# A two-block transformer kernel: first weight panels of the feed-forward part and of the layers in buffers of their own, third layer panel loaded right behind the first

## What is computed

```python
def first_block(x, ...):
    mix = _token_mixer(_rms_norm(h, pre_mix_g), w_in, ..., w_out)
    h = h + _rms_norm(mix, post_mix_g)
    ffn = _channel_mixer(_rms_norm(h, pre_ffn_g), w_up, ffn_conv_w, ffn_conv_b, w_down)
    return h + _rms_norm(ffn, post_ffn_g)

def _channel_mixer(hn, w_up, ffn_conv_w, ffn_conv_b, w_down):
    f = jnp.einsum('btd,df->btf', hn, w_up)            # 1024 -> 2 * 2816
    f = _causal_dwconv(f, ffn_conv_w) + ffn_conv_b
    gate, up = jnp.split(f, 2, axis=-1)
    return jnp.einsum('btf,fd->btd', jax.nn.gelu(gate) * up, w_down)

def second_block(x, ...):
    for l in range(2):
        h = _rms(x, norm_g[l])
        proj = h @ w_in[l]      # gq gk gv ga gz bq bk bv iq ik iw bz cq ck cv cz gate
        ...                     # linear attention, top-k attention, differential attention
        x = x + merged @ w_out[l]
```

## Time and profile before

| | |
|---|---|
| median of 3 runs | 1924.64 us (1924.58 to 1929.13) |
| profiled execution | 1927.01 us, its span 1925.3 us |
| granted TensorE clock, mean of the span | 0.999 |
| TensorE busy | 98% of the span |
| VectorE, ScalarE busy | 60%, 39% |
| from HBM | 157.59 MB, 83 GB/s over the span |

### The profile page before, as it was taken

How to read it: one execution, slowest core, us unless ns; L and a number is a source line. 1 busy time by engine, 2 the same in 40 slices (tenths; PEclk the granted TensorE clock), 3 DMA queues, 4 the chain that set the end, 5 groups by cost and what they waited for, 6 DMA issues and landing times.

```text
span 1925.3 us, 30380 instructions
## 1 busy us (share of the span) xinstructions
PE 1891.2 (98%) x12689; PEld 1533.5 (80%) x12689; DVE 1159.2 (60%) x1725; ACT 750.9 (39%) x1088; POOL 32.0 (2%) x72
## 2 busy tenths in 40 slices
PE   8999999999999999999999999999999999999999
PEld 5677879888888888787777788888787777778887
DVE  5855565776674363547687944545446678864534
ACT  5633333422222254433444334334533445334421
POOL 3000000110000000000000000000000000000000
PEclk9999999999999999999999999999999999999999
DMA  4211014233333322222223222332222222222232
GB/s 155 92 57 47 25 47 132 80 96 104 94 92 105 110 77 88 73 81 88 66 66 109 69 75 66 99 121 77 88 68 87 77 66 78 92 83 66 66 110 88
DMA packets 166020, 161.65 MB, mean 84 GB/s; under 512 B 13876, under 2 KB 150362, under 8 KB 165882
## 3 DMA queue, kind: packets, MB, share of 16 engines
q1 hardware_dynamic: 165184, 158.99, 26.4%
q10 hardware_dynamic: 698, 0.71, 0.1%
HBM read 157.59 MB, written 2.10 MB: 83 GB/s over the span
## 4 chain that ended last, share of the span: by engine, by line
PE 78%; DVE 2%; ACT 1%; issue 0%; ACTq 0%; DVEq 0%
PE psum L617 64%; PE psum L2128 6%; PE psum L2623 2%; PE psum L2600 1%; PE psum L607 1%; PE psum L2580 1%; PE psum L2608 1%; PE psum L533 1%; DVE w_lo L403 1%; PE psum L542 0%; ACT w_hi L352 0%; PE psum L2704 0%; DVE h_lo L467 0%; PE psum L2689 0%; DVE w_lo L384 0%; PE psum L2657 0%
## 5 line engine op out<-in xcount | busy, mean ns | idle before, releaser
L617 PE MATMUL psum<-h_hi,w_hi 128*128 128x512 f32 (+1 forms) x1568 | 608.2, 388 | 10.9 <-DVE h_lo L467 6.3
L617 PE MATMUL psum<-h_lo,w_hi 128*128 128x512 f32 (+1 forms) x1568 | 594.4, 379 | 0.0
L617 PE MATMUL psum<-h_hi,w_lo 128*128 128x512 f32 (+1 forms) x1568 | 594.4, 379 | 0.0
L403 DVE TENSOR_TENSOR w_lo<-w_raw,w_hi 128x2048 fp32r<-128x2048 f32 (+1 forms) x142 | 297.1, 2092 | 283.0 <-ACT w_hi L352 280.5
L352 ACT ACTIVATE w_hi<-w_raw 128x2048 fp32r<-128x2048 f32 (+1 forms) x142 | 249.3, 1756 | 366.2 <-PE psum L617 295.8
L617 PEld LDWEIGHTS psum<-h_hi,w_hi 128*128 128x128 f32 x1568 | 294.4, 188 | 88.6 <-issue 16.3
L617 PEld LDWEIGHTS psum<-h_hi,w_lo 128*128 128x128 f32 x1568 | 294.5, 188 | 55.8
L617 PEld LDWEIGHTS psum<-h_lo,w_hi 128*128 128x128 f32 x1568 | 294.7, 188 | 52.4
L617 PE MATMUL psum<-w_hi,h_hi 128*128 128x512 f32 (+1 forms) x512 | 183.0, 357 | 0.0
L617 PE MATMUL psum<-w_lo,h_hi 128*128 128x512 f32 (+1 forms) x512 | 179.0, 350 | 0.0
L617 PE MATMUL psum<-w_hi,h_lo 128*128 128x512 f32 (+1 forms) x512 | 178.9, 349 | 0.0
(11 more groups left out here) (371 smaller groups left out, 2203.9 us busy)
## 6 DMA issues: line engine op xcount, KB each, us to landing
w_raw<-in_w_in_dram SPq DMA_DIRECT2D x170, 512.0 KB, 4.4
w_raw<-in_w_up_dram SPq DMA_DIRECT2D x44, 512.0 KB, 5.0
w_raw<-in_w_out_dram SPq DMA_DIRECT2D x24, 512.0 KB, 4.6
w_raw<-in_w_br_dram SPq DMA_DIRECT2D x48, 256.0 KB, 3.0
w_raw<-in_w_down_dram SPq DMA_DIRECT2D x22, 512.0 KB, 4.4
x_first<-in_x_dram SPq DMA_DIRECT2D x4, 512.0 KB, 5.5
x_tokens<-in_x_dram SPq DMA_DIRECT2D x4, 512.0 KB, 4.8
out_dram<-x_tokens SPq DMA_DIRECT2D x4, 512.0 KB, 2.6
```

Of the source, the lines that this page charges most:

```text
L403: eng.eng.tensor_tensor(m.wl[:, g % 2, 0:n], m.raw[:, g % 2, 0:n], m.wh[:, g % 2, 0:n].bitcast(F32), ALU.subtract).then_inc(eng.done, 1)
L617: last = pe.eng.matmul(out, a(k), b(k), start=(opens and k == 0 and i == 0), stop=(k == kt - 1 and i == 2), skip_group_check=ks is not None)
```

## The change

It gives the first panels of the feed-forward part and of each layer buffers of their own, in SBUF areas that other tiles have left by then.

- Feed-forward part, panels 0 and 1: `up_raw`, `up_hi`, `up_lo` (raw and lo share their place). They are loaded behind the mixer's last w_out panel and split between the mixer's last steps, by two new functions, `spare_hi` and `spare_lo`. TensorE does the transposes of tiles 2 and 3 before the last output tile of panel 1 instead of behind it.
- Feed-forward part, panels 2 and 3: loaded as soon as w_out panels 16 and 17 are split; panel 2 is split at the end of the seam, panel 3 behind the first gelu.
- Layers, panels 0, 1 and 2: `first_raw`, `spare_hi`, `spare_lo`. The loads are issued in the order 0, 2, 1. For the first layer all three are split around the last two down panels; for the second layer in the seam, at the places where panels 0 and 1 were split before, and panel 2 behind them in one piece.
- Layers, panels 3 and 4 are loaded into the common slots that the previous part's last panels have left, and split right behind the seam.
- First layer: `iq[1]` (panel 2) is also done in two halves, the first behind the transposes of tiles 2 and 3. In both layers its PSUM banks are 3 and 5 instead of 0 and 1.

```diff
+def spare_hi(act, first, g, i):
+    raw, hi, _ = first[i]
+    act.wait_ge(*act.point(("w raw", g + i)))
+    act.wait_ge(act.done, act.so_far())
+    act.eng.activation(hi[:, :], raw[:, :], ACT.Copy).then_inc(act.done, 1)
+    act.counted(("w hi", g + i))
...
             if p == NP - 1:
+                E.wait_ge(pe_done, E.at(("score 23 mm", TT - 1)))
+                E.wait_ge(pe_done, E.at(("score 1 mm", TT - 1)))
+                E.wait_ge(pe_done, E.at(("turn bk", TT - 1, 1)))
+                for i in range(2):
+                    if i:
+                        E.wait_ge(pe_done, E.at(("y mm", 2 * TT - 1)))
...
+                    E.moved(("w raw", NP + i), f"up_loaded{i}", 2)
                 E.wait_ge(dve_done, E.at(("mix", TT - 1)))
...
         y_root(TT - 1)
+        spare_hi(E, m.first_up, NP, 0)
         mix_hi(1, 3, 3, 4)
+        spare_hi(E, m.first_up, NP, 1)
         split_hi_halves(E, m, 16, KT * PW)
         split(17)
...
         mix_lo(1, 3, 3, 4, (3,))
+        spare_lo(E, m.first_up, NP, 0)
         split_lo_halves(E, m, NPROJ + 2, KT * PW)
         split(NPROJ + 3)
+        spare_lo(E, m.first_up, NP, 1)
...
-        for p in range(FT):
-            E.wait_ge(*E.point(("w lo", base + p - 2)))
+        for p in range(2, FT):
+            E.wait_ge(*E.point(("w lo", base + p - (4 if p < 4 else 2))))
...
                 E.wait_ge(*E.point(("w lo", base + p)))
-                for i in range(2):
-                    up(p, i, tt, half == 1)
-            if half == 0:
-                seam_turn(E, m, banks, seam, 2)
-                seam_turn(E, m, banks, seam, 3)
+                up(p, 0, tt, half == 1)
+                if half == 0 and p == 1:
+                    seam_turn(E, m, banks, seam, 2)
+                    seam_turn(E, m, banks, seam, 3)
+                up(p, 1, tt, half == 1)
...
+            if kk == DN - 2:
+                E.wait_ge(dve_done, E.at(("g lo", 7)))
+                for i in (0, 2):
+                    spare_hi(E, m.first, down_base + DN, i)
         split_hi_halves(E, m, down_base + DN - 1, PANEL)
+        spare_hi(E, m.first, down_base + DN, 1)
...
+    def slot_user(p):
+        return base + p - {3: 4, 4: 6}.get(p, 2)
...
+        if p == iq[1]:
+            return 3 + 2 * i
...
-        for p in range(NP):
-            E.wait_ge(*E.point(("w lo", base + p - 2)))
+        for p in (0, 2, 1, *range(3, NP)):
+            if p == 0 and l == 0:
+                E.wait_ge(dve_done, E.before(None, ("G", FT - 1)))
+            if p == 0 and l:
+                E.wait_ge(dve_done, E.before(l - 1, ("dsa lo", NH - 1)))
+            if p >= 3:
+                E.wait_ge(*E.point(("w lo", slot_user(p))))
...
                 panel(lows, half=1)
+                panel(iq[1], half=1 if seam.post is not None else None)
...
                 seam_turn(E, m, banks, seam, 3)
-        panel(iq[1])
+                panel(iq[1], half=0)
```

111 lines of the change are left out of this document (83 added, 28 removed).

## The result

| | before | after | ratio of the runs, 95% interval |
|---|---|---|---|
| first chip, median | 1924.73 us (4 runs) | 1910.97 us (4 runs, 1909.74 to 1911.81) | 0.9915, 0.9904 to 0.9927 |
| second chip, median | 1929.13 us (13 runs) | 1912.66 us (4 runs) | 0.9917, 0.9902 to 0.9932 |
| third chip, median | 1928.34 us (7 runs) | 1912.21 us (4 runs) | 0.9918, 0.9903 to 0.9933 |

A forecast was written before the change was run, and what follows sets the result against it. TensorE, busy 98% of the span, was taken as the bound, with at most 34 us in waits. 4.7 + 0.5 + 6.3 + 1.7 = 13.2 us, less 0.2, from the median of 1924.64 gave 1911.6 us; range 1909.0 to 1915.5.

The forecast's parts named there:

- First seam, 4.7 + 0.5 us: Mixer to feed-forward: second half starts at 356.87 instead of 361.61 (4.7 us); the third panel's wait goes (0.5 us).
- the very slack of the prediction: First seam: h_lo there at 356.68, TensorE's second half at 356.87, so in time by 0.2 us.
- Second seam, 6.3 us: Feed-forward to first layer: four waits go (5.5 us), the clock's fall goes (1.5 us), halving the third panel costs 0.7 us.
- The halving: First layer's third panel: 96 matmuls of 256 columns instead of 48 take 11.7 instead of 10.9 us; cost taken as 0.7 us.
- The 0.2 us taken off: Taken from the sum of 13.2 us for switches between blocks that stay a little slow, leaving 13.0 us.
- The low end: Range's lower end, 1909.0 us: halving at 0.1 us, 0.3 us per removed wait, 0.4 us between median and span.
- Third seam, 1.7 us: First to second layer: waits of 0.42 + 0.16 and 0.98 + 0.16 us go, 1.7 us in all.
- it did not fall after the same 2.50 us: First seam: TensorE's clock was taken not to fall behind the h_lo wait, so no gain was counted for it there.
- The norm chain: Rival, 12%: at the first seam the norm chain doesn't run ahead, second half 1.2 us later; about 1913.2 us.
- The clock fell nowhere else: Answers a rival, 5%: the low clock falls somewhere else all the same and costs its 1.5 us; 1913.1 us.
- The change took effect: Answers a rival, 3%: splits still end behind the norm work, only 0.5 + 1.1 + 1.7 us come; 1921.3 us.
- Loads in a row: Rival, 7%: layer panels landing after 687.3 us delay the last down panel one for one; landing at 691 gives 1915.3 us.

The follow-up runs named there:

- whole_third: The changed kernel with the first layer's third panel computed whole behind the transposes instead of half on each side of them; 1916.69 us.
- layers_only: The changed kernel with the feed-forward entry of before, so only the layers' part of the change; 1918.66 us, ratio 0.9949 to before.
- turns_only: The kernel before with only the 16 transposes of tiles 2 and 3 moved ahead of up panel 1's last tile; 1925.68 us.

## Why the prediction came out as it did

The waits went as forecast. What failed are sizes in the sum: three terms for how TensorE walks between the waits (1.6 us together), and the fall of the clock in the first seam, which was put at nothing and cost 1.4 to 1.5 us in two of four profiled executions of before.

**First seam, 4.7 + 0.5 us: mechanism right, 0.8 us too small.** As forecast, no wait is left, and h_lo is ready with little to spare: 353.35 + 0.14 is 0.2 us ahead of the second half at 353.70, the very slack of the prediction. The mis-sized term is the walk of TensorE between the waits. I took 48 matmuls at 5.86 us, a number from a block that starts behind a wait and therefore slowly; in the changed kernel the blocks follow without a stop, and 96 matmuls take 11.36 us (353.70 to 365.06), 0.118 us each. From the first transposes to the second half it is 17.7 us where 18.2 was forecast (22.9 before), and to the third panel 29.1 where the terms give 29.8 (35.0 before). So the term of 4.7 us measured 5.2, and the one of 0.5, the third panel's wait, measured 0.8, because the block behind that wait started slowly too.

**Second seam, 6.3 us: 0.6 too small.** The four waits went and the clock stayed at 1.00, both as forecast. The halving was mis-sized: I compared two unequal starts and got 0.7 us (5.86 / 48 with a slow start, against a panel without one). The panel of before started behind its own wait and took 11.15 us (739.74 to 750.89); 96 halves in a row at 0.1195 take 11.5. TensorE's first instruction behind that panel, in before:

```profile
750.89 0.23 PE L607 MATMUL psum<-ident,layer_rows 13*128 13x13 f32 x1
```

That is 0.3 us, and whole_third gives the same. The other 0.2 us of the 0.6 were not taken apart. The Trainium skill (TensorE: Matmul & The Clock Gate, section Back-to-back issue gap) would have had this term nearer, at 0.12 us, by its formula for an isolated matmul, though that formula's gap for 256 columns (0.109 us) is below every stretch here.

**The 0.2 us taken off** for switches between blocks that stay a little slow had the wrong sign for the same reason. These three are in the main one mistake: a wait costs more than its bracket, because the block behind it also starts slowly. 0.8 + 0.6 + 0.2 = 1.6 us, the whole of the difference between 13.0 and 14.6. The low end held these costs (the halving at 0.1 us, 0.3 us per removed wait) and the 0.4 us between median and span, 2.6 us in all; they came to 1.6. The falls of the clock in the first seam, for which it held nothing, add 0.7 us on average. That makes 15.3 us, or 1909.3 us, still inside the range. The last 1.0 us down to the 1908.4 of the ratio isn't placed by any run; the stretch before 300 us, which stays open, is as large (1.0 to 1.1 us between the groups).

**Third seam, 1.7 us: right**, 1.7 to 1.8 in all eight profiles that have the layers' part.

**The clock.** That it fell behind the second seam's waits and would stay up when they went was right, and layers_only shows it alone. What failed is the sentence that at the first seam "it did not fall after the same 2.50 us": one execution was read as a rule. It falls there in two of four profiled executions of before, and each that has it gains 1.4 to 1.5 us more from the change. On the first chip, three of the four runs of before lie at 1924.6 to 1924.8, 2.3 us under the profiled one, which had one fall; they probably had fewer, but their clocks were not recorded, so this is argued. It would explain why the gain in the medians is 13.8 us there and 16 on the other chips: 14.6 + half of 1.5 + what stays open before 300 us. In the changed kernel no profile shows a fall before the end of the span. But two of its twelve executions, both without a profile (1911.81 and 1912.79 us), have a mean granted clock of 0.998, lower than with one fall (0.999 over the profile of before); where it was low in them is not known.

**Rivals.** The norm chain was not the bound: it ran ahead as far as thought. The clock fell nowhere else in the three profiles of the changed kernel; for the two executions just named this is open. The change took effect. Loads in a row: the price (8.0 us from the landing, then one for one) is confirmed by two kernels, but I had misjudged how near it was. The landing was put at 683.9 us of the trace of before, with 3.4 us to spare until 687.3; in after it is 677.59 + 8.73 (how far after is ahead there) = 686.3, with 1.0 us to spare. The best GB/s of one microsecond, 422, was taken for the rate of the whole block; from 673 to 676 us the trace of after has a mean of 349 GB/s (length, TensorE busy, granted clock, DMA share, GB/s):

```profile
673.00:676.00 3.00, 3.00 (x15) 1.00 1.10 349
```

The Trainium skill (DMA: Bandwidth & Descriptors, section Specifications) gives about 358 GB/s, which put the landing at 685.2: here its figure was the better guide than the row that I chose against it. The chance of 7% for this rival was too small for a margin of 1 us.

## What to carry to other kernels

A wait that disappears gives back more than its bracket: the slow start of the block behind it, and, for the waits of 1.9 us and more seen here, a fall of TensorE's clock that only some executions show; so price a seam from several profiles, and streaming matmuls from a stretch without a stop. Own buffers help only if the split that they allow is moved out of the seam, as well as its load. Where an in-order engine must split a panel that is still in flight, look for the landing time, for everything else in the issuing queue (a panel that came behind 14 small loads, 5.8 us of the queue, landed 7.8 us later here), and for what stands behind that split; the peak rate of one microsecond says little of when a block lands.

## What the runs showed of the hardware

- TensorE's clock went to 1.2 GHz after single stops of 1.89 us (turns_only) and 2.50 us (whole_third), but not in every execution: in four of ten profiles at the first seam, in eleven of eleven at the second. A fall cost 1.4 to 1.6 us behind a wait of 1.9 to 2.5 us and 1.7 to 2.2 us behind one of 6.6 to 7.6 us. What makes the first seam differ from the second was not tried. The Trainium skill (TensorE: Matmul & The Clock Gate, section HAM oscillation — how this bites in real kernels) tells of waits that let the clock down so that the next block starts cold. The traces agree that this happens; the stops after which it happened here are shorter than the waits of the page's example.
- Matmuls of 256 columns stream at 0.118 to 0.1195 us each, and the one behind a set of transposes or a stop is followed only after 0.20 to 0.23 us (350.75 to 350.95 in after, 351.35 to 351.58 in before).
- Three chips gave medians of the kernel before that differ by 4.4 us (1924.7 to 1929.1), and of the changed one by 1.7.
